# Where one block's weights are rounded and split inside the attention steps of a two-layer streaming encoder

## The reference, cut to what matters

```python
q, k, v = diff_project(h, diff_w_in[j], diff_q_norm[j], diff_k_norm[j])
...
s = jnp.einsum('bqhcd,bkhcd->bhcqk', q_blk, k).astype(jnp.float32) * scale
p = jax.nn.softmax(jnp.where(mask, s, -jnp.inf), axis=-1)
a = p[:, :, 0] - lam * p[:, :, 1]
return jnp.einsum('bhqk,bkhe->bqhe', a.astype(v.dtype), v)
...
o = rms_norm(o, diff_norm[j]) * (1.0 - lam_init)
mix = jnp.einsum('bthe,hed->btd', o, diff_w_out[j].reshape(DIFF_HEADS, DIFF_DV, D_MODEL))
```

## Time and profile before

| what | value |
|---|---|
| median of 3 runs | 1411.09 us (1410.72 to 1411.91) |
| the profiled execution's own time | 1414.2 us |
| its span in the trace | 1412.1 us |
| PE busy | 1379.7 us (98%) |
| DVE busy | 950.9 us (67%) |
| ACT busy | 654.9 us (46%) |
| granted TensorE clock, mean | 0.996 of full |
| DMA | 182.42 MB, mean 129 GB/s |

### The profile page before, as it was taken

How to read it: one execution, slowest core, us unless ns; L and a number is a source line. 1 busy time by engine, 2 the same in 40 slices (tenths; PEclk the granted TensorE clock), 3 DMA queues, 4 the chain that set the end, 5 groups by cost and what they waited for, 6 DMA issues and landing times.

```text
span 1412.1 us, 26324 instructions
## 1 busy us (share of the span) xinstructions
PE 1379.7 (98%) x10896; PEld 1299.6 (92%) x10896; DVE 950.9 (67%) x1591; ACT 654.9 (46%) x1456; POOL 89.2 (6%) x149
## 2 busy tenths in 40 slices
PE   8999999999999999999999999999999999999999
PEld 6878878999999999999988787879899999999999
DVE  4587786569988788778665546466888654554554
ACT  4543343356554354252565565644565552552530
POOL 0000000210000000000300000000300000000000
PEclk9999999999999999999999999999999999999999
DMA  9644533244444544535433234112334223223223
GB/s 381 219 157 146 176 135 113 68 139 159 151 157 142 182 142 147 174 120 167 155 134 105 78 109 148 63 40 82 120 123 146 91 71 110 90 68 113 75 65 106
DMA packets 37583, 182.42 MB, mean 129 GB/s; under 512 B 4247, under 2 KB 6423, under 8 KB 26073
## 3 DMA queue, kind: packets, MB, share of 16 engines
q1 hardware_dynamic: 22552, 126.98, 26.0%
q0 software_dynamic: 14912, 53.78, 11.1%
HBM read 172.82 MB, written 7.91 MB: 128 GB/s over the span
## 4 chain that ended last, share of the span: by engine, by line
PE 86%; DVE 6%; ACT 4%; issue 2%; DMA 1%; POOL 0%; SPq 0%; DVEq 0%; ACTq 0%; POOLq 0%
PE ps L644 26%; PE ps L646 25%; PE ps L645 25%; DVE sq L1676 1%; ACT w_hi L1129 1%; PE ps L1030 1%; DVE h_lo L1689 1%; PE ps L1071 1%; PE ps L989 1%; PE ps L1049 1%; PE ps L729 1%; PE ps L882 1%; PE ps L878 1%; DVE w_lo L1604 1%; PE ps L682 1%
## 5 line engine op out<-in xcount | busy, mean ns | idle before, releaser
L646 PE MATMUL ps<-h_hi,w_lo 128*128 128x272 f32 x2080 | 602.3, 290 | 0.0
L644 PE MATMUL ps<-h_hi,w_hi 128*128 128x272 f32 x1984 | 579.7, 292 | 6.4 <-ACT up L1403 1.7
L645 PE MATMUL ps<-h_lo,w_hi 128*128 128x272 f32 x1984 | 571.3, 288 | 0.0
L646 PEld LDWEIGHTS ps<-h_hi,w_lo 128*128 128x128 f32 x2080 | 391.7, 188 | 0.0
L644 PEld LDWEIGHTS ps<-h_hi,w_hi 128*128 128x128 f32 x1984 | 374.1, 189 | 17.9 <-issue 8.1
L645 PEld LDWEIGHTS ps<-h_lo,w_hi 128*128 128x128 f32 x1984 | 374.6, 189 | 1.0 <-issue 1.0
L1129 ACT CAST w_hi<-w_raw 128x2048 fp32r<-128x2048 f32 (+2 forms) x108 | 183.0, 1695 | 196.9 <-PE ps L646 169.1
L1604 DVE TENSOR_TENSOR w_lo<-w_raw,w_hi 128x2048 fp32r<-128x2048 f32 (+2 forms) x106 | 219.6, 2071 | 71.0 <-ACT w_hi L1129 70.4
L645 PE MATMUL ps<-act_lo,w_hi 128*128 128x272 f32 (+1 forms) x704 | 203.8, 290 | 0.0
L644 PE MATMUL ps<-act_hi,w_hi 128*128 128x272 f32 (+1 forms) x704 | 203.5, 289 | 0.0
L646 PE MATMUL ps<-act_hi,w_lo 128*128 128x272 f32 (+1 forms) x704 | 203.2, 289 | 0.0
(11 more groups left out here) (266 smaller groups left out, 1735.9 us busy)
## 6 DMA issues: line engine op xcount, KB each, us to landing
w_raw<-in_wst SPq DMA_DIRECT2D x73, 1024.0 KB, 5.0
a_raw<-in_ada_r POOLq DMA_DIRECT2D x56, 512.5 KB, 4.3
w_raw<-in_wst SPq DMA_DIRECT2D x28, 768.0 KB, 4.3
a_raw<-in_ada_g POOLq DMA_DIRECT2D x24, 512.0 KB, 3.7
a_pro<-in_ada_w SPq DMA_DIRECT2D x8, 1024.0 KB, 18.1
v_raw<-in_wst SPq DMA_DIRECT2D x8, 1024.0 KB, 8.7
w_raw<-in_wst SPq DMA_DIRECT2D x8, 512.0 KB, 3.8
xT<-in_xT SPq DMA_DIRECT2D x4, 544.0 KB, 6.9
```

Of the source, the lines that this page charges most:

```text
L644: mm(out, lhs_hi, rhs_hi, start=first, stop=False)
L645: mm(out, lhs_hi, rhs_lo, start=False, stop=False)
L646: return mm(out, lhs_lo, rhs_hi, start=False, stop=last)
```

## The change

In the attention steps three things move, and nothing is computed otherwise. ACT no longer rounds a block when its last unit is evacuated, but at the end of the step, behind `values_out`, and always the whole block. DVE's `low` of an owed block is cut in two halves of columns; the first stands where `low` stood, the second behind the evacuation of the step's last unit. In steps without a unit (step 8 of pairs 0 to 2) DVE does `weights_out(gu)` between `combined(gu+1)` and `maxima(gu+2)`, no longer behind the maxima.

```diff
--- before.py
+++ after.py
@@ -1549,11 +1549,15 @@
                         heads_turned(p - 1, i - 1, 7)
                     for idx in NORM_FIRST.get(i, []):
                         head_norms(p + 1, idx)
-                    if len(todo[i]) > 1:
-                        evacuate(todo[i][0])
+                    owed = None
+                    for u in todo[i][:-1]:
+                        evacuate(u, False)
+                        owed = UNITS[u][0] + 2 if u == LAST_U[UNITS[u][0]] else owed
                     exps(gu + 2)
                     for u in todo[i][-1:]:
-                        evacuate(u, not (last and i == NU - 1))
+                        evacuate(u, False)
+                        if u == LAST_U[UNITS[u][0]] and not (last and i == NU - 1):
+                            owed = UNITS[u][0] + 2
                     if last and i == NU - 2:
                         split(BN[("doutB", 0)])
                     for idx in NORM_THEN.get(i, []):
@@ -1561,6 +1565,8 @@
                     if last and i == 2:
                         heads_turned(p - 1, 2, 7)
                     values_out(gu)
+                    if owed is not None:
+                        split(owed)
                 output_roots(p)
             heads_turned(NPAIR - 1, 0, 4)
             heads_turned(NPAIR - 1, 1, 5)
@@ -1594,14 +1600,17 @@
             step = Steps(dve, dve_step)
             TT, STT = dve.tensor_tensor, dve.scalar_tensor_tensor
 
-            def low(n):
+            def low(n, part=None):
                 if n >= NB:
                     return
                 m = block_kt(n) * BC
                 dve.wait_ge(w_hi_ok, n + 1)
                 if n:
                     dve.wait_ge(w_lo_ok, n)
-                TT(low_cols(w_lo, n, 0, m), low_cols(w_raw, n, 0, m), f32(hi_cols(n, 0, m)), ALU.subtract).then_inc(w_lo_ok, 1)
+                c0, c1 = (0, m) if part is None else (part * m // 2, (part + 1) * m // 2)
+                ins = TT(low_cols(w_lo, n, c0, c1), low_cols(w_raw, n, c0, c1), f32(hi_cols(n, c0, c1)), ALU.subtract)
+                if part != 0:
+                    ins.then_inc(w_lo_ok, 1)
 
             def ada_add(i):
                 l, b = ADA_ORDER[i]
@@ -2111,6 +2120,9 @@
                 for i in range(NU):
                     gu = NU * p + i
                     combined(gu + 1)
+                    alone = not todo[i]
+                    if alone:
+                        weights_out(gu)
                     maxima(gu + 2)
                     if p and i == 0:
                         outputs_normalised(p - 1)
@@ -2119,17 +2131,21 @@
                     for u in todo[i][:-1]:
                         evacuate(u, False)
                         owed = UNITS[u][0] + 2 if u == LAST_U[UNITS[u][0]] else owed
-                    weights_out(gu)
+                    if not alone:
+                        weights_out(gu)
                     if p and 1 <= i < (3 if last else 4):
                         heads_low(p - 1, i - 1, 7)
                     if last and i == NU - 1:
                         low(BN[("doutB", 0)])
-                    elif owed is not None:
-                        low(owed)
-                        owed = None
+                    behind = None
+                    if not (last and i == NU - 1) and owed is not None:
+                        low(owed, 0)
+                        behind, owed = owed, None
                     for u in todo[i][-1:]:
                         evacuate(u, False)
                         owed = UNITS[u][0] + 2 if u == LAST_U[UNITS[u][0]] else owed
+                    if behind is not None:
+                        low(behind, 1)
                     for idx in NORM_THEN.get(i, []):
                         heads_normalised(p + 1, idx)
                     if last and i == 2:
```

## The result

| what | before | after |
|---|---|---|
| median of the runs | 1412.06 us (1410.72 to 1414.71, 6 runs) | 1419.60 us (1418.46 to 1425.09, 6 runs) |
| ratio to before | | 1.006, 95% interval 1.0048 to 1.0071 |
| profiled execution's own time | 1414.2 us | 1423.34 us |
| its span | 1412.1 us | 1421.2 us |
| granted TensorE clock, mean | 0.996 | 0.993 |

The kernel became slower by 7.5 us by the medians, where 5.2 were forecast; 1419.6 lies above the range. The direction and the places were right, the sum was 2.3 us short. The other 1.0 us between the forecast 1416.3 and 1419.6 is the base: the forecast was added to 1411.09, the median of three runs of before, and that of six is 1412.06.

The account below looks back on a forecast made before the run. PE, busy 98% of the span, was taken as the bound, so only its waits count. Losses of 3.66 + 1.85 + 1.5 = 7.0 us less 1.8 gained gave 5.2 slower: 1411.09 to 1416.3 us, range 1413.0 to 1418.5.

Parts of the forecast that it names:

- The gains: Pairs 0 to 2: shorter waits in steps 6 and 8, less 0.3 us in pair 0's step 2; 1.8 us gained.
- Pair 2: End of pair 2: no gain, since pair 3's first transpose already waits for ACT's values_out, which doesn't move.
- A1's wait: Pair 3, step 2: unit A1 waits for the last head's low part, 3.66 us of idle PE.
- What comes behind A1's wait: Pair 3, step 3: combined, maxima and copy fit in, the copy done 1.2 us before the values need it.
- Rival (d): Tight places of pairs 1 and 2 tip over: 1.7 us more, 1418.0 us; chance 0.13.
- rival (a): The gaps go and nothing takes their place: about 3.7 us faster, 1407.4 us; chance 0.05.
- The second loss: Pair 3, step 5: values due at 962.66 start at 964.50, behind DVE's copy; 1.85 us lost.
- The third loss: Pair 3, step 7: values due at 974.43 start at 975.94, behind DVE's copy; 1.5 us lost.
- DVE's own wait: Sign in pair 3: DVE's wait for ACT's rounding ahead of the low part grows by some 3 to 4 us.
- The rule that spoke for the halves: Skill's rule that breaking up instructions may help; by it the kernel comes out as in (a); prediction sided against it.
- (b): Only the wait for the head's low part costs, copies are covered: 1.9 us slower, 1413.0 us; chance 0.10.
- (c): A1 is held less, by 1.9 us, its wait met another way: 3.4 us slower, 1414.5 us; chance 0.12.

Follow-up runs that it names:

- the rounding alone: Kernel before, with only ACT's rounding moved behind the values of the step; DVE's low part whole, copy as before: +7.18 us in the trace, ratio 1.0048.
- the copy alone: Kernel before, with only DVE's copy of the turned weights moved ahead of the maxima in steps without a unit: +0.14 us in the trace, ratio 1.0001.
- Halves alone: Kernel before, with only DVE's low part cut in two halves; ACT's rounding and the copy stay: -0.07 us in the trace, ratio 0.9999.
- the 30 products: Changed kernel, with PE doing 30 unused small matmuls into A1's bank just ahead of A1: +9.73 us in the trace against before, ratio 1.0087.
- head's low part first: Changed kernel, with the last head's low part ahead of the block's in pair 3's step 2: +3.51 us in the trace against before, ratio 1.0021.
- the parts that pay: Kernel before, late rounding only at step 5 of pairs 0 to 2, some copies ahead of maxima, one values_out ahead of exponentials: -4.01 us, ratio 0.9968.

## Why the prediction was right in kind and short in size

**What bounds the kernel: right.** Only PE's waits and speed could change the time, and all of it happened between the first and the last attention step.

**The gains: right in sum.** Pair 0 was given 0.8, pair 1 1.05, pair 2 nothing, together 1.8. Measured: 0.70, 1.07 and -0.05, together 1.72. In pair 0 the late start in step 2 cost 0.35 (0.3 in the working), and step 4, given as covered, nothing. From there to the values of step 6 it gained 0.80 (0.78), and in step 8 0.24 (0.32). The waits behind the copy that were forecast as 0.3 to 0.4 are there, 0.22 in step 6 and 0.38 in step 8:

```profile
794.09 0.94 PE L1071 MATMUL ps<-vd,aT 128*128 128x128 f32 x6 [0.22 <-DVE aT L2083]
...
801.24 0.49 PE L1071 MATMUL ps<-vd,aT 128*128 128x128 f32 x2 [0.38 <-DVE aT L2083]
```

**Pair 2: right number, wrong reason.** The prediction said that ACT's `values_out`, for which pair 3's first transpose waits, doesn't move, and for step 8 that the maxima don't move. With the rounding alone pair 2 gains 0.74; with the copy alone it loses 0.79, because there the maxima do move. The two make the 0.05 of after. The zero was the sum of two things of which neither was in the working.

**A1's wait: right.** 3.66 us by the working, 3.66 in the trace. The halves took 0.96 and 0.95 where 0.94 was taken, and followed each other as counted.

**What comes behind A1's wait: the step that failed.** The effect of the clock behind this wait was put at nothing without a reason. The sum counts "3.66 us of idle PE" and then goes on as if PE resumed at the speed that it had. It resumed at half, and that cost 2.57 us. Nothing else is missing: 3.66 + 1.81 + 1.54 + 0.10 - 1.72 = 5.39, to which the clock's 2.57 and 0.07 at the same site add up to the 8.03. With PE kept busy through the wait, the total was 5.38. The profile of before had no idle time of this length in the stretch (its longest wait of PE for ACT there was 1.0), so its granted clock of 1.00 in every window of the earlier trace rows said nothing on what a new one of 3.66 would do. But outside the stretch the same trace shows what an idle time can do. Behind a wait of 1.79 us in layer 0 PE works at half for 3.4 us (a row, and the window of PE behind it: stretch, length, PE busy, granted clock, DMA share, GB/s), and behind one of 4.21 us near 15 us it does so too:

```profile
129.07 0.73 PE L836 MATMUL ps<-alT,w_alpha 33*128 33x272 f32 x4 [1.79 <-DVE oT L1886]
```

```profile
130.05:133.40 3.35, 3.35 (x17) 0.50 0.00 0
```

The matmuls there start 0.227 us apart and not 0.126, so 3.4 us at half cost about 1.5 (an estimate from these rows). The clock should have been a term with bounds: nothing at one end, and at the other all of A1 and what follows at half speed for as long as it lasts. Such a term would have carried the upper end of the range to the measured time. Rival (d) was the only case above the forecast, and it was about something else. Nor does the range's end of 1418.5 follow from its terms: (d) alone gives 1418.0, the six halves at their upper bound 1417.9, both 1419.6. And the gains of rival (a) add up to 3.5, not 3.7.

**The second loss: right.** 1.85 by the working, 1.81 measured, with the idle time where it was put:

```profile
969.42 0.68 DVE L2083 COPY aT<-ps 128x512 f32<-128x512 f32 x1
970.15 1.16 PE L1071 MATMUL ps<-vd,aT 128*128 128x128 f32 x8 [1.37 <-DVE aT L2083]
```

The values show 1.37 idle and not 1.8. Another 0.27 had been lost at unit A6, which starts only when the evacuation of A4 between the halves ends (966.27 for 965.72 + 0.49); the prediction had said that A6 adds nothing. The remaining 0.17 us are start spacing of PE that the profile doesn't call idle.

**The third loss: right in size (1.54 for 1.5), wrong in place.** The prediction said that A10, whose bank waits for the evacuation between the halves, is held for less than the values of step 7 and adds nothing. A10 is what shows the wait, and the values come right behind their copy without one of their own:

```profile
979.59 0.96 DVE L1611 TENSOR_TENSOR w_lo<-w_raw,w_hi 128x768 fp32r<-128x768 f32 x1 [4.20 <-ACT w_hi L1129]
...
981.02 0.39 PE L644 MATMUL ps<-od_hi,w_hi 128*128 128x272 f32 x1 [1.09 <-DVE xT L1774]
...
983.00 0.41 DVE L2083 COPY aT<-ps 128x256 f32<-128x256 f32 x1
...
983.46 0.71 PE L1071 MATMUL ps<-vd,aT 128*128 128x128 f32 x4
```

**DVE's own wait.** DVE stands idle ahead of the halves, for ACT's rounding, for 4.21 us in step 2, 5.45 in step 4 and 4.20 in step 6. The prediction named a growth of 3 to 4 us as its sign (0.35 in the earlier trace rows); the sign is there, and larger.

**The rule that spoke for the halves.** The Trainium skill, Perfetto Trace Analysis, section Optimizing Scalar/DVE Operations, says that breaking up instructions "may allow work to be completed sooner" where ACT or DVE aren't saturated but hold others. Halves alone gave -0.07 us. The prediction had set it aside because both halves still stand ahead of what PE waits for. That held for A1 and the copies. It did not hold for A10, which waits for the evacuation between the halves: there they gave 0.7 us beside the late rounding.

**The rivals.** (a), all gaps go, is refuted by the three waits. (b), only the head's low part costs, is refuted by the 1.81 and 1.54 of the other two sites, and (c), a shorter wait of A1, by the 3.66. (d), pairs 1 and 2 tip over, is refuted too: they gained 1.02.

## What to carry to other kernels

A step that is moved to the end of its engine's turn delays every engine that waits for it, and what stands behind that wait in the second engine's order: here 64 columns of low part, 0.28 us of work, held TensorE for 3.66. Look for such small pieces with a waiting reader first, and put them ahead of the wait: that alone was worth 4.5 of the 8 us. And when a change puts an idle time into a TensorE that had none there, add a term for the clock behind it, with both ends. A stretch in which the clock never fell can't exclude it; look for a fall in the rest of the profile, where this one had two. A late rounding paid only where a transpose was seen to wait for ACT and nothing of DVE's was late by it.

## What the hardware showed that I had not expected

- The length of an idle time alone doesn't tell whether the clock falls. It fell to 0.50 behind 3.66 us (cost 2.57 us) and 3.60 us (cost 1.59 us), and stayed at 1.00 behind 1.33, 1.37, 1.55 and 1.89 us in the attention steps. But six of the kernels have the same wait of 1.32 or 1.33 us at pair 3's first transpose, and in one of the six executions, that of the 30 products, it was followed by 0.50. A wait of 1.37 or 1.38 us stands between 1003 and 1019 us in all ten traces, and the clock fell behind it in two of them (head's low part first, and the parts that pay), at a cost of 0.6 us each. And before has a fall behind 1.79 us. What decides between these, no run here shows. The windows behind the 1.37 in after, and behind the 1.89 (unit A10) with the rounding alone:

```profile
970.10:975.00 4.90, 4.85 (x39) 4.61 (x40) 2.47 (x9) 1.10 (x6) 0.00 (x0) 1.00 0.00 0
```

```profile
976.30:980.00 3.70, 2.97 (x22) 2.78 (x22) 2.01 (x7) 0.64 (x3) 0.00 (x0) 1.00 0.00 0
```

- Nearly the same wait cost differently by the clock: with the rounding alone PE ran its first matmuls of A1 at full speed and fell afterwards, in after it resumed at half and stayed there longer. Since the clock differs among executions with the same wait, this needn't be a difference between the kernels; it was not tried.
- 15 products of no use, in a time in which PE would have waited anyway, made the kernel 2.65 us faster in the trace, and 1.6 us by the medians over before, a difference that the intervals don't secure.
